# The second half's down-projection as seven-product pairs: three layers of a transformer-like encoder step on one Trainium2 core

## Chip, cores and metric

One NeuronCore of one Trainium2 chip runs the whole program. The metric is the device time of one execution in microseconds (us). TensorE (PE) multiplies, VectorE (DVE) and ScalarE (ACT) prepare its operands and read its results, GpSimd (POOL) adds a few squares, and SyncE (SP) issues nearly all transfers. Each engine works through its own queue in program order and waits on semaphores.

## The reference

Four layers over 512 prompt tokens and 32 sample tokens (544 rows of width 1024), in float32. Each layer has a token mixer (gated linear attention, band attention, a recurrent block, gated linear attention), then a SwiGLU feed-forward part; both add to x:

```python
def rmsnorm(x, g):
    y = xf * lax.rsqrt(jnp.mean(xf * xf, axis=-1, keepdims=True) + EPS)
    return (y * g.astype(jnp.float32)).astype(x.dtype)

def swiglu_ffn(x, w_in, w_out):          # w_in 1024 x 5632, w_out 2816 x 1024
    g, u = jnp.split(x @ w_in, 2, axis=-1)
    return (jax.nn.silu(g) * u) @ w_out
...
for i in range(DEPTH):                   # 4 layers
    ...                                  # xp = xp + mixer(rmsnorm(xp))
    xp = xp + swiglu_ffn(rmsnorm(xp, ffn_norms[i]), *ffn_params[i])
    xs = xs + swiglu_ffn(rmsnorm(xs, ffn_norms[i]), *ffn_params[i])
y_prompt = rmsnorm(xp, final_norm)
```

## The kernel before

**Layout.** Activations lie transposed: x is 8 tiles of 128 features by 544 tokens, a token row being two halves of 272 columns. Every matmul has a 128x128 weight tile and 272 columns. A product in float32 is made of three: each operand is split into a high part and a low rest, and hi*hi, hi*lo and lo*hi are added up. ACT writes the high part of weights (`w_hi`), DVE the low one (`w_lo`).

**The feed-forward part.** The 22 tiles of the hidden width are done in two halves of FH = 11: up-projection of half 0 (`up0`), down-projection (`down0`), then `up1` and `down1`. h is the product silu(g) * u; ACT writes `h_hi`, DVE `h_lo`. `up1` is made of eleven "seven" pairs already: a pair (u and g of one hidden tile) is a 2x2 matrix product over 2x4 input tiles and two column halves, done in Winograd's form, with 7 products of KQ = 4 tiles instead of 8. It needs sums of weight tiles (`w_sums` on DVE, then `lo_sums`, `lo_a11`, `lo_more_sums`, `lo_rest`; `hi_...` on ACT) and sums of input tiles (`t_sum`, `t_low` on DVE, `t_high` on ACT), made once for the layer. `h_low` stands in DVE's queue behind `product`, which waits for ACT's silu.

**The down-projection.** `project_out` does 8 blocks, one for each tile m of x, of 11 tiles x 3 products x 2 halves = 66 matmuls. Block b writes `slot[b % 2]` in PSUM. Ahead of a block ACT and DVE split its weights (`split`, L772 and L1483); behind it DVE multiplies by rstd (L2133), adds to x (L2136), ACT squares x (L790) and writes `xg_hi` (L775), POOL adds up the squares (L3031), and DVE writes `xg_lo` (L1495). Behind the eighth block DVE adds the last square (`last_square`, L1490), and PE's next block, the first of the next mixer, stops after six of its eight input tiles for the ten small matmuls of `stat_sum` (L2466), which wait for that sum. In the layer ahead of the second gated linear attention this first block has 4 matmuls a tile (L2422), elsewhere 6 (L2414).

**Queues.** A block's `pe.wait_ge(s_free, b - 1)` keeps PE from writing a PSUM slot that is not yet read; the semaphores are counters, so an engine that is late in its queue holds up all that waits for a later count. Weights come by SP through two `raw` buffers (and `ffn_raw_b` for every other pair).

## Time and profile before

| | |
|---|---|
| median of 3 runs | 2532.9 us (2532.87 to 2533.35) |
| profiled execution, its own time | 2532.84 us |
| its span (first to last instruction) | 2531.1 us |
| around the span | 1.7 us |
| PE busy | 2513.2 us (99%), 19925 matmuls |
| DVE busy | 1749.3 us (69%) |
| ACT busy | 1210.6 us (48%) |
| POOL busy | 166.1 us (7%) |
| share of PE in the chain that ended last | 96% |

The span is the profiler's, from the first to the last instruction of that one execution; a difference in its time is a difference in the median as far as the two agree, here within 0.1 us. Busy shares are means over stages that have different limits.

### The profile page before, as it was taken

What the parts mean: (1) busy time and instruction counts of PE and PEld (TensorE: products, weight loads), DVE (VectorE), ACT (ScalarE), POOL (GpSimd) and SP (SyncE); (2) the same over time, 40 slices, a digit from 0 to 9 for tenths busy, and PEclk for the clock granted to TensorE, in tenths of its full rate; (3) what the DMA queues carried; (4) which work ended last, traced back from release to release, by engine and by line L of the source; (5) the groups of instructions that cost most, each with busy time, mean ns of one, the idle gap of its engine ahead of it and who ended that gap; (6) DMA issues with size and microseconds to landing.
All of it is one profiled execution on the core that took longest, in us unless ns stands there. A gap on an engine that the chain in (4) does not pass through costs nothing.

```text
span 2531.1 us, 48151 instructions
## 1 busy us (share of the span) xinstructions
PE 2513.2 (99%) x19925; PEld 2451.8 (97%) x19925; DVE 1749.3 (69%) x2585; ACT 1210.6 (48%) x1831; POOL 166.1 (7%) x180
## 2 busy tenths in 40 slices
PE   9999999999999999999999999999999999999998
PEld 8999999999988899999998899999999999999998
DVE  6655994985555599489557557948955565984973
ACT  6554651543555565245245545524534554642543
POOL 1101000001000010000122110000011101000001
PEclk9999999999999999999999999999999999999999
DMA  4222333332433233333222233332323223333332
GB/s 120 71 78 84 101 101 91 100 97 82 120 96 110 71 109 95 97 97 94 85 68 74 72 92 90 103 100 84 96 82 88 72 70 92 108 89 93 106 88 78
DMA packets 443891, 230.69 MB, mean 91 GB/s; under 512 B 17092, under 2 KB 440736, under 8 KB 443696
## 3 DMA queue, kind: packets, MB, share of 16 engines
q1 hardware_dynamic: 442048, 226.90, 31.2%
q8 instruction: 140, 2.29, 0.4%
q10 hardware_dynamic: 1200, 0.59, 0.1%
q0 software_dynamic: 448, 0.45, 0.1%
q14 instruction: 55, 0.45, 0.1%
HBM read 219.03 MB, written 8.87 MB: 90 GB/s over the span
## 4 chain that ended last, share of the span: by engine, by line
PE 96%; DVE 2%; issue 1%; ACT 0%; DMA 0%; POOL 0%; SPq 0%; DVEq 0%; ACTq 0%; POOLq 0%
PE slot L2414 32%; PE slot L2457 21%; PE aux L2934 6%; PE aux L2929 6%; PE aux L2931 6%; PE slot L2934 5%; PE slot L2929 5%; PE slot L2931 5%; PE aux L2373 2%; PE aux L2827 1%; PE aux L2582 1%; PE aux L2833 1%; PE aux L2739 1%; PE aux L2677 1%; PE aux L2597 1%
## 5 line engine op out<-in xcount | busy, mean ns | idle before, releaser
L772 ACT ACTIVATE w_hi<-raw 128x1024 fp32r<-128x1024 f32 (+3 forms) x207 | 239.5, 1157 | 266.1 <-PE slot L2457 136.4
L2414 PE MATMUL slot<-xg_hi,w_hi 128*128 128x272 f32 x1664 | 361.5, 298 | 2.9 <-DVE w_lo L1483 2.9
L2414 PE MATMUL slot<-xg_lo,w_hi 128*128 128x272 f32 x1664 | 343.8, 288 | 0.0
L2414 PE MATMUL slot<-xg_hi,w_lo 128*128 128x272 f32 x1664 | 343.7, 288 | 0.0
L1483 DVE TENSOR_TENSOR w_lo<-raw,w_hi 128x1024 fp32r<-128x1024 f32 (+4 forms) x207 | 281.6, 1360 | 61.1 <-ACT w_hi L772 59.3
L2414 PEld LDWEIGHTS slot<-xg_hi,w_hi 128*128 128x128 f32 x1664 | 260.4, 189 | 14.1 <-issue 6.9
L2414 PEld LDWEIGHTS slot<-xg_lo,w_hi 128*128 128x128 f32 x1664 | 261.5, 189 | 0.0
L2414 PEld LDWEIGHTS slot<-xg_hi,w_lo 128*128 128x128 f32 x1664 | 260.4, 189 | 0.0
L2133 DVE TENSOR_TENSOR ffn_y<-slot,rstd 128x544 f32<-128x544 f32 x56 | 40.6, 724 | 194.1 <-PE slot L2457 177.9
L3031 POOL TENSOR_TENSOR sq_sum<-sq_sum,sq_x 128x544 f32<-128x544 f32 x48 | 67.9, 1414 | 1608.5 <-ACT sq_x L790 1608.2
L2457 PE MATMUL slot<-h_hi,w_hi 128*128 128x272 f32 x1078 | 150.0, 287 | 0.0
L2457 PE MATMUL slot<-h_hi,w_lo 128*128 128x272 f32 x1078 | 149.8, 287 | 0.0
L2457 PE MATMUL slot<-h_lo,w_hi 128*128 128x272 f32 x1078 | 149.8, 287 | 0.0
L790 ACT ACTIVATE sq_x<-x 128x544 f32<-128x544 f32 (+1 forms) x55 | 36.2, 658 | 222.3 <-DVE x L2136 119.4
L2457 PEld LDWEIGHTS slot<-h_hi,w_hi 128*128 128x128 f32 x1078 | 140.5, 188 | 0.0
L2457 PEld LDWEIGHTS slot<-h_lo,w_hi 128*128 128x128 f32 x1078 | 140.1, 188 | 0.0
L2457 PEld LDWEIGHTS slot<-h_hi,w_lo 128*128 128x128 f32 x1078 | 140.0, 188 | 0.0
L2934 PE MATMUL aux<-ffn_t_hi,w_lo 128*128 128x272 f32 x704 | 116.7, 287 | 0.0
L1311 ACT ACTIVATE w_hi<-ffn_w_sums 128x1024 fp32r<-128x1024 f32 x80 | 85.0, 1063 | 66.0 <-DVE ffn_w_sums L2170 64.9
L2929 PE MATMUL aux<-ffn_t_hi,w_hi 128*128 128x272 f32 x704 | 116.6, 287 | 0.0
L2931 PE MATMUL aux<-ffn_t_lo,w_hi 128*128 128x272 f32 x704 | 116.6, 287 | 0.0
L1329 ACT ACTIVATE w_hi<-ffn_w_sums 128x1024 fp32r<-128x1024 f32 x80 | 85.0, 1063 | 62.1 <-PE aux L2934 29.6
(421 smaller groups left out, 5763.3 us busy)
## 6 DMA issues: line engine op xcount, KB each, us to landing
raw<-in_l_ffn_w_out_dram SPq DMA_DIRECT2D x64, 704.0 KB, 4.6
raw<-in_l_ffn_w_in_dram SPq DMA_DIRECT2D x52, 512.0 KB, 5.0
raw<-in_l_gla_w_in_dram SPq DMA_DIRECT2D x47, 512.0 KB, 3.8
ffn_raw_b<-in_l_ffn_w_in_dram SPq DMA_DIRECT2D x88, 256.0 KB, 3.4
ffn_raw_b<-in_l_ffn_w_in_dram SPq DMA_DIRECT2D x44, 512.0 KB, 5.2
raw<-in_l_ffn_w_in_dram SPq DMA_DIRECT2D x72, 256.0 KB, 3.3
raw<-in_l_att_w_qkv_dram SPq DMA_DIRECT2D x24, 512.0 KB, 3.7
raw<-in_l_lru_w_in_dram SPq DMA_DIRECT2D x24, 512.0 KB, 3.8
```

What stands on the lines that cost most here:

```text
L772: act.activation(w_hi[par][:, 0:kt, :], raw[par][:, 0:kt, :], ACT.Copy).then_inc(s_hi, 1)
L1311: act.activation(tiles8(w_his, w_slots(b % 2)[0]), tiles8(FF["s"], 0), ACT.Copy).then_inc(s_wh, 1)
L1329: act.activation(tiles8(w_his, min(w_slots(b % 2)[2:4])), tiles8(FF["s"], 2 * KQ), ACT.Copy).then_inc(s_wh, 1)
L1483: dve.tensor_tensor(w_lo[par][:, 0:kt, :], raw[par][:, 0:kt, :], w_hi[par][:, 0:kt, :].bitcast(F32), ALU.subtract).then_inc(s_lo, 1)
L2133: dve.tensor_tensor(FF["y"][:, 2 * j:2 * j + 2, :], slot[(p0 + j) % 2][:, :, 0:HALF], halves(rstd[:, :]), ALU.mult).then_inc(s_free, 1)
L2373: return pe.transpose(out, in_, ident[rows, rows])
L2414: ins = pe.matmul((slot[par] if bank is None else bank)[:, hf, 0:HALF], w[par][:, k, :], a[:, k0 + k, hf * HALF:(hf + 1) * HALF], start=(k ...
L2457: ins = pe.matmul(to[:, hf, 0:HALF], w[par][:, k, :], a[:, k, cols], start=(k == 0 and at == 0), stop=(k == kt - 1 and at == 2))
L2929: pe.matmul(to, w_his[:, w_at + k, :], hi(k), start=(start and k == 0), stop=False, skip_group_check=True)
L2931: pe.matmul(to, w_his[:, w_at + k, :], lo(k), start=False, stop=False, skip_group_check=True)
L2934: ins = pe.matmul(to, w_los[:, w_at + k, :], hi(k), start=False, stop=(stop and k == KQ - 1), skip_group_check=True)
L3031: pool.tensor_tensor(sq_sum[:, :], sq_sum[:, :], sq_x[par][:, :], ALU.add).then_inc(s_xad, 1)
```

## The change

In layers 0, 1 and 2 the second half's down-projection (`down1`) keeps blocks 0 and 1 as they are and does blocks 2 to 7 as three seven-product pairs (blocks 2+3, 4+5, 6+7). Of the 11 hidden tiles KX = 3 are multiplied plainly and the other 8 in Winograd's form. Its input sums are made of h itself, so `product` leaves the seven h tiles 3 to 9 in float32 in places that are free in `up1` (`whole_h`), and tile 10 in `ffn_y`. All three pairs use the same two PSUM slots; the rests of the weights (`extra`) lie in the last two tiles of `xg_hi` and `xg_lo`.

```diff
+H_SUM_AT, T_DVE, T_ACT = (0, 3, 7, 11), 32, 12
+DOWN_PAIRS = (2, 4, 6)
+KX = FH - XT
...
             # ScalarE
+            def project_seven(i, b0):
...
+                split(b0 + 1, 1 - p0, FH)
+                t_half(i, 0)
+                t_half(i, 1)
+                t_half(i, 2)
+                hi_sums(pairs[0], b2, None)
+                t_half(i, 3)
+                hi_more_sums(pairs[0], b2, None)
+                hi_extra(pairs[0], b2)
+                hi_a11(pairs[0], b2, None)
+                hi_rest(pairs[0], b2)
+                copy_product(pairs[0], p0, "d")
+                copy_product(pairs[0], p0, "b")
+                x_ready(0)
+                x_ready(1)
...
+                copy_product(pairs[2], p0, "b")
+                x_ready(4)
+                x_ready(5)
+                split(b0 + 8, p0, next_k(i, "down1"))
+                x_ready(6)
+                x_ready(7)
...
             # VectorE
+            def down_ends(at, b):
+
+                n, ab = s_no[at], up_banks(at[1], at[2], b % 2)[1]
+                dve.wait_ge(s_mm, b + 2)
+                dve.wait_ge(s_out7, 5 * n + 3)
+                dve.tensor_tensor(FF["y"][:, 3, :], ab[:, 1, 0:HALF], down_v[:, :], ALU.add).then_inc(s_out7, 1)
+                dve.tensor_tensor(FF["y"][:, 0, :], ab[:, 0, 0:HALF], rstd[:, 0:HALF], ALU.mult).then_inc(s_free, 1)
+                dve.wait_ge(s_out7, 5 * n + 4)
+                dve.tensor_tensor(FF["y"][:, 2:4, :], FF["y"][:, 2:4, :], halves(rstd[:, :]), ALU.mult).then_inc(s_out7, 1)
...
+            def h_sum(i, q):
+
+                at, tq = T_DVE * i + 16 + H_SUM_AT[q], FF["hs"][:, :, q, :]
+                top, low = whole_h(i, 1, KX + q), whole_h(i, 1, KX + KQ + q)
+                dve.tensor_tensor(tq[:, 1, :], low[:, 1, :], top[:, 1, :], ALU.subtract)
+                dve.tensor_tensor(tq[:, 0, :], top[:, 0, :], top[:, 1, :], ALU.subtract).then_inc(s_tdve, 1)
+                dve.wait_ge(s_tdve, at + 1)
+                dve.scalar_tensor_tensor(tq[:, 2, :], low[:, 1, :], -1.0, tq[:, 0, :], ALU.mult, ALU.subtract).then_inc(s_tdve, 1)
+                dve.wait_ge(s_tdve, at + 2)
+                dve.scalar_tensor_tensor(tq[:, 3, :], tq[:, 2, :], -1.0, low[:, 0, :], ALU.mult, ALU.subtract).then_inc(s_tdve, 1)
...
+                split(b0 + 1, 1 - p0, FH)
+                h_sum(i, 0)
+                h_sum(i, 1)
+                h_sum_low(i, 0)
+                h_sum(i, 2)
+                h_sum_low(i, 1)
+                h_sum(i, 3)
+                h_sum_low(i, 2)
+                w_sums(pairs[0], b2)
+                h_sum_low(i, 3)
+                lo_sums(pairs[0], b2)
+                scaled(0, b0)
+                lo_more_sums(pairs[0], b2, 2)
+                scaled(1, b0 + 1, 2)
+                lo_extra(pairs[0], b2)
+                lo_a11(pairs[0], b2, 3)
+                c_plus_d(pairs[0], p0)
+                lo_rest(pairs[0], b2)
+                added(0, b0)
+                added(1, b0 + 1, 2)
+                a_plus_b(pairs[0], p0)
+                low(0)
+                low(1)
+                w_sums(pairs[1], b2 + 2)
+                down_middle(pairs[0], b2)
+                lo_sums(pairs[1], b2 + 2)
+                lo_a11(pairs[1], b2 + 2, 2)
+                lo_more_sums(pairs[1], b2 + 2, 3)
+                down_ends(pairs[0], b2)
+                lo_rest(pairs[1], b2 + 2)
+                lo_extra(pairs[1], b2 + 2)
+                c_plus_d(pairs[1], p0)
+                down_adds(pairs[0], b2)
+                low(2)
+                low(3)
+                a_plus_b(pairs[1], p0)
...
+                split(b0 + 8, p0, next_k(i, "down1"))
+                down_middle(pairs[2], b2 + 4)
+                down_ends(pairs[2], b2 + 4)
+                down_adds(pairs[2], b2 + 4)
+                low(6)
+                last_square(norm_no(i, "down1"))
+                low(7)
...
             # TensorE
+            def seven_of_down(i, j):
...
+                pe.wait_ge(s_free, b - 1)
+                pe.wait_ge(s_tdve, T_DVE * i + 32)
+                pe.wait_ge(s_wh, 3 * n + 1)
+                times(c, slots[0], *of_t(0), True, (s_wl, 3 * n + 1))
+                times(d_, slots[1], *of_t(1), True, (s_wl, 3 * n + 1)).then_inc(s_pr, 1)
+                pe.wait_ge(s_wh, third)
+                pe.wait_ge(s_free, b)
+                times(b_, slots[2], *of_t(2), True, (s_wl, third)).then_inc(s_mm, 1)
+                pe.wait_ge(s_wh, 3 * n + 3)
+                times(a, slots[4], *of_h(KX, 0), True, (s_wl, 3 * n + 3)).then_inc(s_pr, 1)
+                pe.wait_ge(s_out7, 5 * n + 1)
+                times(c, slots[3], *of_h(KX + KQ, 1), False, (s_wl, 3 * n + 3)).then_inc(s_pr, 1)
+                pe.wait_ge(s_hi, b + 2)
+                pe.wait_ge(s_lo, b + 2)
+                rest_of(c, 0, 1, False)
+                times(d_, slots[5], *of_t(3), False, (s_lo, b + 2))
+                rest_of(d_, 1, 0, False).then_inc(s_pr, 1)
+                pe.wait_ge(s_out7, 5 * n + 2)
+                times(a, slots[6], *of_h(KX + KQ, 0), False, (s_lo, b + 2))
+                rest_of(a, 0, 0, False)
+                rest_of(b_, 1, 1, True).then_inc(s_mm, 1)
```

`times` is 3 x 4 matmuls and `rest_of` 3 x 3, so a pair has 7 x 12 + 4 x 9 = 120 where two blocks have 132. `scaled(m)` is the multiplication by rstd, `added(m)` the addition to x, `low(m)` the write of `xg_lo`, `x_ready(m)` ACT's square and `xg_hi`. SP loads a pair's weights by three transfers and a fourth for the rests.

VectorE's queue between the h of the last up pair and the first read of block 0 (layer 0, `down1`; `h_sums` hold the sums of h). Before:

```order
L2256 TENSOR_TENSOR h_lo<-ffn_y,h_hi 128x544 [waits h_hi]
L2144 UNCONDITIONAL_BRANCH
L2144 ISA
L1483 TENSOR_TENSOR w_lo<-raw,w_hi 128x1408 [waits w_hi]
L2129 REGISTER_ALU
L2133 TENSOR_TENSOR ffn_y<-slot,rstd 128x544 [waits block_done]
```

Now, the last rows ahead of that read (the fourth `h_sum`, then `w_sums`, `h_sum_low(3)`, `lo_sums`, `scaled(0)`):

```order
L2398 TENSOR_TENSOR ffn_h_sums<-ffn_y,whole_in_xg_lo 128x272
L2399 TENSOR_TENSOR ffn_h_sums<-whole_in_xg_lo 128x272
L2401 SCALAR_TENSOR_TENSOR ffn_h_sums<-ffn_y,ffn_h_sums 128x272 [waits t_dve]
L2403 SCALAR_TENSOR_TENSOR ffn_h_sums<-ffn_h_sums,ffn_y 128x272 [waits t_dve]
L2408 TENSOR_TENSOR ffn_t_lo<-ffn_h_sums,ffn_t_hi 128x4x272 [waits t_act]
L2304 TENSOR_TENSOR ffn_w_sums<-ffn_raw_b 128x1024 [waits seven_raw_b_in]
L2307 TENSOR_TENSOR ffn_w_sums<-ffn_w_sums,ffn_raw_b 128x512 [waits seven_w_sums]
L2309 TENSOR_TENSOR ffn_w_sums<-ffn_w_sums,ffn_raw_b 128x512 [waits seven_w_sums]
L2408 TENSOR_TENSOR ffn_t_lo<-ffn_h_sums,ffn_t_hi 128x4x272 [waits t_act]
L2315 TENSOR_TENSOR w_lo<-ffn_w_sums,w_hi 128x1024 [waits seven_w_hi]
L2421 TENSOR_TENSOR ffn_y<-slot,rstd 128x544 [waits block_done]
```

Between the weight split and the first read of a PSUM slot there were no rows of work; now there are 24.

ScalarE's queue at the same place (the copy behind the h of the last up pair, then the split of block 1's weights). Now:

```order
L1495 ACTIVATE h_hi<-ffn_y 128x544 [waits ffn_h]
L840 ACTIVATE w_hi<-raw 128x1408 [waits block_done,raw_in0]
L1419 ACTIVATE ffn_t_hi<-ffn_h_sums 128x4x272 [waits t_dve] x3
L1379 ACTIVATE w_hi<-ffn_w_sums 128x1024 [waits block_done,seven_w_sums]
L1419 ACTIVATE ffn_t_hi<-ffn_h_sums 128x4x272 [waits t_dve]
L1397 ACTIVATE w_hi<-ffn_w_sums 128x1024 [waits block_done,seven_w_sums]
```

Before, the square of x stood directly behind the split; now the fourth copy of the h sums stands behind a copy that waits for VectorE's weight sums.

## Rows read from the trace of the kernel before

**Rows 1.** The page, part 1: busy time, share of the span and instructions.

```profile
PE 2513.2 (99%) x19925; PEld 2451.8 (97%) x19925; DVE 1749.3 (69%) x2585; ACT 1210.6 (48%) x1831; POOL 166.1 (7%) x180
```

**Rows 2.** Chain that ended last, in order of time: start us, us, what.

```profile
556.19 8.25 PE slot L2414 x66
564.44 57.41 PE slot L2457 x462
```

**Rows 3.** The same chain in 545 to 640 us, two of its pieces.

```profile
546.23 0.50 PE aux L2931 x4
...
555.21 0.49 PE aux L2931 x4
```

**Rows 4.** Timeline of DVE, 555 to 640 us: start us, us, engine line op.

```profile
559.26 0.73 DVE L2256 TENSOR_TENSOR h_lo<-ffn_y,h_hi 128x544 fp32r<-128x544 f32 x1 [0.72 <-ACT h_hi L1363]
560.53 1.63 DVE L1483 TENSOR_TENSOR w_lo<-raw,w_hi 128x1408 fp32r<-128x1408 f32 x1 [0.54 <-ACT w_hi L772]
```

**Rows 5.** Timeline of DVE, 252 to 300 us (`t_sum`, `t_low`, `w_sums`, `lo_sums` in `up0`).

```profile
268.63 0.72 DVE L2266 TENSOR_TENSOR ffn_tq<-ffn_xq 128x544 f32<-128x544 f32 x1
269.39 0.44 DVE L2269 SCALAR_TENSOR_TENSOR ffn_tq<-ffn_xq,ffn_tq 128x272 f32<-128x272 f32 x1
...
270.22 0.72 DVE L2266 TENSOR_TENSOR ffn_tq<-ffn_xq 128x544 f32<-128x544 f32 x1
...
274.26 2.50 DVE L2276 TENSOR_TENSOR ffn_t_lo<-ffn_tq,ffn_t_hi 128x1088 fp32r<-128x1088 f32 x2
276.67 1.22 DVE L2170 TENSOR_TENSOR ffn_w_sums<-ffn_raw_b 128x1024 f32<-128x1024 f32 x1
...
279.25 0.72 DVE L2340 TENSOR_TENSOR ffn_y<-slot,rstd 128x544 f32<-128x544 f32 x1
279.89 1.22 DVE L2181 TENSOR_TENSOR w_lo<-ffn_w_sums,w_hi 128x1024 fp32r<-128x1024 f32 x1
```

**Rows 6.** Timeline of ACT, 252 to 300 us: a copy of input sums, one of weight sums.

```profile
262.83 1.12 ACT L1379 ACTIVATE ffn_t_hi<-ffn_tq 128x1088 fp32r<-128x1088 f32 x1 [0.59 <-DVE ffn_tq L2271]
...
277.92 1.06 ACT L1311 ACTIVATE w_hi<-ffn_w_sums 128x1024 fp32r<-128x1024 f32 x1 [2.70 <-DVE ffn_w_sums L2170]
```

**Rows 7.** The page, part 6: transfers, KB each, us from issue to landing.

```profile
ffn_raw_b<-in_l_ffn_w_in_dram SPq DMA_DIRECT2D x44, 512.0 KB, 5.2
```

**Rows 8.** Timeline of DVE, 555 to 640 us, behind the last block of `down1`.

```profile
621.89 0.72 DVE L2133 TENSOR_TENSOR ffn_y<-slot,rstd 128x544 f32<-128x544 f32 x1 [2.86 <-PE slot L2457]
...
624.10 0.73 DVE L1490 TENSOR_TENSOR sq_sum<-sq_sum,sq_x 128x544 f32<-128x544 f32 x1 [0.72 <-ACT sq_x L790]
```

**Rows 9.** Timeline of ACT there: the last square and the last `xg_hi`.

```profile
623.41 0.66 ACT L790 ACTIVATE sq_x<-x 128x544 f32<-128x544 f32 x1 [5.95 <-DVE x L2136]
623.97 0.73 ACT L775 ACTIVATE xg_hi<-x,vec_a 128x544 fp32r<-128x544 f32 x1
```

**Rows 10.** Timeline of POOL, 540 to 650 us: its last addition of squares.

```profile
615.94 1.36 POOL L3031 TENSOR_TENSOR sq_sum<-sq_sum,sq_x 128x544 f32<-128x544 f32 x1 [6.46 <-ACT sq_x L790]
```

**Rows 11.** Timeline of PE, 619 to 650 us: `stat_sum`.

```profile
626.20 1.17 PE L2466 MATMUL aux<-mean_x,sq_sum 128*128 128x1 f32 x10
```

**Rows 12.** Stages: us, PE, PEld, DVE, ACT, POOL busy (x), PEclk, DMA share, GB/s.

```profile
572.60:621.70 49.10, 49.10 (x398) 49.10 (x397) 25.01 (x24) 15.10 (x18) 8.20 (x6) 1.00 0.30 85
...
2525.00:2528.00 3.00, 0.53 (x5) 0.29 (x4) 1.11 (x3) 1.56 (x3) 0.00 (x0) 0.80 0.37 113
2528.00:2531.00 3.00, 0.00 (x0) 0.00 (x0) 0.00 (x0) 0.00 (x0) 0.00 (x0) 0.50 0.74 294
```

**Rows 13.** Timeline of PE at the program's start and at its end.

```profile
4.73 0.24 PE L2373 MATMUL slot<-ident,gain_rows 8*128 8x8 f32 x1 [4.73 <-DMA x_rows<-in_x_sample_dram]
...
10.55 0.65 PE L2414 MATMUL slot<-xg_lo,w_hi 128*128 128x272 f32 x2
11.00 0.49 PE L2414 MATMUL slot<-xg_hi,w_lo 128*128 128x272 f32 x2
...
2522.48 0.28 PE L2891 MATMUL slot<-h_hi,w_lo 128*128 128x256 f32 x1
```

More of the change, by code:

```diff
@@ L178, in up_plan @@
                     n += 1
+        for j in range(len(DOWN_PAIRS) if i < layers - 1 else 0):
+            number[i, "down", j], buffer[i, "down", j] = n, "BA"[j % 2]
+            n += 1
     return number, buffer, h_count
@@ L1294, in raw_used @@
                     for par in range(2):
[L1295 removed]
+                        raw_off[par] -= 0 if at[1] == "down" and par == b % 2 else 16
                 else:
@@ new lines, in h_sum_low, with project_seven, scaled, added @@
+            def h_sum_low(i, q):
+                dve.wait_ge(s_tact, T_ACT * i + 8 + q + 1)
+                dve.tensor_tensor(one4(FF["t_lo"], q), one4(FF["hs"], q), one4(FF["t_hi"], q).bitcast(F32),
+                                  ALU.subtract).then_inc(s_tdve, 1)
+            def project_seven(i, b0):
+                p0, norm = b0 % 2, norm_after(i, "down1")
+                b2, pairs = b0 + DOWN_PAIRS[0], [(i, "down", j) for j in range(len(DOWN_PAIRS))]
+                def scaled(m, b, at=0):
+                    dve.wait_ge(s_mm, b + 1)
+                    if m > 1:
+                        dve.wait_ge(s_xd, XT * (2 * i + 1) + m)
+                    dve.tensor_tensor(FF["y"][:, at:at + 2, :], slot[b % 2][:, :, 0:HALF], halves(rstd[:, :]), ALU.mult).then_inc(s_free, 1)
+                def added(m, b, at=0):
+                    dve.wait_ge(s_free, b + 1)
+                    dve.tensor_tensor(one(x, m), FF["gu"[at // 2]], one(x, m), ALU.add).then_inc(s_xd, 1)
+                def add(m, b):
+                    scaled(m, b)
+                    added(m, b)
+                def low(m):
+                    xg_split(m, norm, m + split_tiles(i, "down1"))
+                split(b0 + 1, 1 - p0, FH)
[34 more added lines that the diff above has]
+                a_plus_b(pairs[1], p0)
+                w_sums(pairs[2], b2 + 4)
+                down_middle(pairs[1], b2 + 2)
+                lo_sums(pairs[2], b2 + 4)
+                lo_a11(pairs[2], b2 + 4, 2)
+                lo_more_sums(pairs[2], b2 + 4, 3)
+                down_ends(pairs[1], b2 + 2)
+                lo_extra(pairs[2], b2 + 4)
+                lo_rest(pairs[2], b2 + 4)
+                c_plus_d(pairs[2], p0)
+                down_adds(pairs[1], b2 + 2)
+                low(4)
+                low(5)
+                a_plus_b(pairs[2], p0)
+                split(b0 + 8, p0, next_k(i, "down1"))
[5 more added lines that the diff above has]
+                low(7)
@@ L2962, in project_out, with project_seven @@
+            def project_seven(i, b0, ready):
+                p0, hi, lo = b0 % 2, FF["h_hi"], FF["h_lo"]
+                mm_block(b0, p0, FH, hi, lo, ready=ready, free=b0 - 2)
+                whole_block(b0 + 1, 1 - p0, FH, hi, lo, free=b0 - 2)
+                for j in range(len(DOWN_PAIRS)):
+                    seven_of_down(i, j)
             def project_out(b0, kt, hi, lo, ready, free=None):
```

207 lines of the change are left out of this document (178 added, 29 removed).

## The prediction

> **What bounds the kernel now.** I read the page's busy shares first: PE is busy for 99% of the span, VectorE for 69%, ScalarE for 48% [rows 1]. Such a share is a mean over stages, so I went to the chain of work that ended last: in layer 0's `down1` it is PE alone, 66 matmuls in 8.25 us and then 462 in 57.41 us, without a piece of any other engine [rows 2]. In that stage VectorE is busy for 25.0 of 49.1 us [rows 12]. So PE's matmuls set the time, and fewer of them are worth their full price, as long as the other engines deliver in time. Whether they do is the question of this change, because it gives VectorE and ScalarE much more to do in exactly this stage, and part of it can't start before the last tile of h is there.
>
> **What PE saves.** A plain block's matmul takes 57.41 / 462 = 0.1243 us. One in the seven-product form takes 0.1247 us: from the piece at 546.23 to that at 555.21 are 18 pieces of 4, 8.98 us for 72 [rows 3]. Two plain blocks are 132 x 0.1243 = 16.40 us. A pair is 84 x 0.1247 + 36 x 0.1243 = 14.95 us (the 36 of `rest_of` priced like plain ones). That saves 1.45 us a pair, and 9 pairs (three in each of three layers) save **13.1 us**.
>
> **What the first pair waits for.** Blocks 0 and 1 have 132 matmuls, so PE could start the first pair at 556.19 + 8.25 + 66 x 0.1243 = 572.6. Its first matmul waits for three things: all 16 tiles of h sums (`s_tdve`), the first weight sums (`s_wh`), and the read of block 0 out of the slot it writes (`s_free`), which is `scaled(0)`. That read stands in VectorE's queue behind all four `h_sum`, all four `h_sum_low`, `w_sums` and `lo_sums`. I walk down that queue with durations of before.
>
> VectorE writes the last `h_lo` at 559.26 and starts the split of block 1's weights at 560.53 [rows 4]. Nothing of this moves earlier. An operation's successor starts about 0.08 us ahead of the end of its record: the one at 279.25, of 0.72, is followed at 279.89 [rows 5]. So the first `h_sum` can start at 562.07.
>
> An `h_sum` is a `t_sum` whose first operation, 544 wide, is cut into two of 272. A `t_sum` takes 1.59 us from start to start, its first part 0.76 of it [rows 5]. Two operations of 272 take 0.36 + 0.48 in its place (0.44 each, the second waited for), which makes 1.67 us. Four are 6.7 us. An `h_sum_low` is a `t_low`: 2.41 us for two, 1.2 each [rows 5]. Three stand ahead of `w_sums`, 3.6 us. ScalarE's copies of 1.12 us [rows 6] fit between, since each has the next `h_sum` to hide under. `w_sums` starts at 562.07 + 6.7 + 3.6 = 572.4, so VectorE alone has already used up the time of blocks 0 and 1.
>
> Then comes the knot. ScalarE's queue has `hi_sums` ahead of the fourth `t_half`. `hi_sums` waits for the first weight sum, 1.22 us behind 572.4, and takes 1.06 [rows 5, 6]: until 574.7. The fourth `t_half` takes 1.12: until 575.7. VectorE has finished `w_sums` by 575.0 and waits; its fourth `h_sum_low` runs to 577.0, `lo_sums` to 578.1 (1.22 less 0.08), and `scaled(0)` ends 0.72 later, at 578.8 [rows 5]. PE starts then, 6.2 us late. Layers 1 and 2 have the same two lists of instructions, so this is 3 x 6.2 = **18.6 us lost**, more than the pairs save. The second and third waits of the first pair (`scaled(1)`, `c_plus_d`, `lo_rest`) come out 1.3 us or more ahead of PE by the same walk.
>
> **What the other pairs wait for.** Loading is not it, I think: the second pair's transfers are issued behind the first pair's `lo_extra` at about 581.4 by the walk, some 6.5 us ahead of its `w_sums`, and such a transfer lands within 5.2 us [rows 7]; the others have more room. Per pair VectorE has, in us by the widths of rows 5: `w_sums` 2.6, `down_middle` 1.5, `lo_sums` with `lo_a11` and `lo_more_sums` 2.9, `down_ends` 1.4, `lo_rest` 1.1, `lo_extra` 0.9, `c_plus_d` and `a_plus_b` 0.7, the additions 1.3, two `xg_lo` 1.5. That is 13.9 of a pair's 14.95 us. It fits, with little air. Walking down the queue, `c_plus_d` of the third pair is the tightest: PE wants it 48 matmuls, 6.0 us, into the pair, and it is ready about 0.6 us earlier, because it stands behind `down_ends`, which can't start before the pair ahead has ended. I take 0 for these waits and keep them as a rival.
>
> **What the next layer waits for.** Before, the eighth block's product is scaled from 621.89 on (call it E), and its square is added by 624.10 + 0.73, E + 2.9 [rows 8]. PE comes to `stat_sum` at 626.20, E + 4.3, so it doesn't wait [rows 11]. Now tiles 6 and 7 of x are both finished behind E. `down_ends` has two operations of 272 and one of 544, then two additions of 544: x6 is there at E + 2.1, x7 at E + 2.7. ScalarE squares x6 until E + 2.8 (0.66), writes its `xg_hi` (0.73) and squares x7 until about E + 4.0 [rows 9]. POOL must add the square of x6, 1.36 us [rows 10], until E + 4.2; before, its last addition was done at 617.30, long ahead. VectorE's `last_square` then ends at E + 5.0. Where PE arrives at E + 4.3 (layers 1 and 2) it waits 0.7 us. Ahead of layer 3 the first block has 4 matmuls a tile and not 6, so PE arrives after 24 and not 36 of them, at E + 3.0, and waits 2.0 us. Together **3.4 us**. The splits for the second block are ready in time in both.
>
> **What TensorE's clock does.** In this trace PE rests nowhere in mid-program, and the granted clock is 1.00, the level of 2.4 GHz, in the stage [rows 12]. It falls at the very end: after the last dense matmul at 2522.48 [rows 13] PE has hardly any work, and the granted clock is 0.80 in 2525 to 2528 and 0.50 (1.2 GHz) from there on [rows 12]. A mean of 0.80 is 0.50 for 1.2 of these 3 us, so it fell about 4.3 us behind the last dense matmul. The new wait of 6.2 us is longer. What comes after such a rest is seen at the start, by durations alone: PE's first work is at 4.73, and the two matmuls at 10.55 are still 0.225 us apart [rows 13], not 0.125; the slow part is over by about 11.3, 6.6 us in. Half of the time at the lower level is lost. So a wait costs from nothing (the clock stays) to 3.3 us more. PE had gaps at the start and will have none here, so I expect a shorter slow part and take 2.0 us, 3 x 2.0 = **6.0 us**. The Trainium skill, page "TensorE: Matmul & The Clock Gate", section on the HAM clock gate, says that the array falls to the lower clock when it idles and gets the higher one back by sustained matmuls. The rows at both ends agree with it. By that page this change pays for each rest twice; without it the sum would be 6.0 us lower.
>
> **Sum.** 18.6 - 13.1 + 3.4 + 6.0 = +14.9 us, **2547.8 us**. The profiled execution has 2532.84 us by its own clock, 1.7 more than its span, and the median is 2532.9, so I add to the median directly.
>
> **Rivals.** About 0.2% (5 us) is what a measurement of this kernel can tell from no change.
> - *The clock stays up* through a rest of 6 us. For: the gap at the end was not quite a rest, with six small matmuls in it, and the level fell only once PE was all but done. Against: the slow start. Time: 2541.8 us. Chance 0.19.
> - *The pairs starve VectorE's queue.* If the 0.6 us of air in `c_plus_d` is not there and the second and third pair each lose 1 us, that is 6 us more: 2554 us. For: 13.9 of 14.95 us. Against: the other waits of a pair have 0.8 to 2 us of air by the same walk. Chance 0.14.
> - *The h sums are hidden* (faster). If VectorE's and ScalarE's chain from 562.07 to `scaled(0)` took 10.5 us in place of 16.7, the first pair would start on time and the time would be 2532.9 - 13.1 + 3.4 = 2523.2 us. It decides at a wait of (13.1 - 3.4) / 3 = 3.2 us a layer; below that, the change gains. For: only that I may have misjudged which operation must be ahead of which; the widths are those of rows 5. Chance 0.08.
> - My forecast, wait and lower clock: 0.57, own range 2543 to 2551.4 (the two ends of the clock's price are 2541.8 and 2551.7). What is left, 0.02, is a wait of half the size.
>
> **Range and chances.** From 2540 us (the clock stays up and VectorE is a little quicker) to 2554 us (the second rival): it leaves out the hidden sums and half of the starved pairs. Slower by over 0.2%, above 2538.0: 0.88. Within 0.2%: 0.04. Faster, below 2527.8: 0.08.
>
> **What will show it.** In the profile after, in each of three layers, PE should have one idle stretch of about 6 us ahead of the first `ffn_t_hi` matmul of `down1`, released by VectorE's read of `slot`; the last of the four copies of h sums on ScalarE should start about 1.1 us after a copy of `w_sums`; the granted clock should be under 1.00 just behind the stretch, with matmuls 0.225 us apart for some 4 us; a pair should then take 14.95 us without a wait; and `stat_sum` should wait 0.7, 0.7 and 2.0 us for `sq_sum`. The count of matmuls must fall by 108. I am wrong if the stretch is under 3.2 us, or if the later pairs are longer than 15.5 us.

## The result, and the profile after

The changed kernel takes 2557.6 us (median of 4 runs, 2556.2 to 2558.1) against 2533.1 us (2532.9 to 2533.4) of the kernel before beside it: a ratio of 1.0096, 95% interval 1.0084 to 1.0108. It is 24.5 us slower. The direction is as forecast, the size is not: 2547.8 us was predicted and 2554 us was the upper end of the range.

The profiled execution has 2558.13 us by its own clock, 25.3 more than the one of before. Its page, part 1, answers to [rows 1]:

```profile
PE 2513.9 (98%) x19817; PEld 2449.7 (96%) x19817; DVE 1841.6 (72%) x2762; ACT 1246.1 (49%) x1897; POOL 167.7 (7%) x180
```

TensorE has 108 matmuls fewer and is not busy for less: at half the clock a matmul is busy for longer. What it waits for, from the view of waits (us in total, times, longest):

```profile
PE slot L3251 <- DVE ffn_y L2421: 18.4, 3, 6.2
...
PE aux L2746 <- DVE sq_sum L1624: 4.6, 3, 2.5
...
PE slot L3251 <- DVE ffn_y L2382: 0.8, 3, 0.3
```

The first row is the wait ahead of the first pair, for `scaled(0)`. The timelines of VectorE, ScalarE and TensorE in layer 0 show what is late there (start us, us, engine line op; for the durations of before see [rows 5] and [rows 6]):

```profile
572.64 1.22 DVE L2304 TENSOR_TENSOR ffn_w_sums<-ffn_raw_b 128x1024 f32<-128x1024 f32 x1
...
575.98 1.29 DVE L2408 TENSOR_TENSOR ffn_t_lo<-ffn_h_sums,ffn_t_hi 128x1088 fp32r<-128x1088 f32 x1 [0.67 <-ACT ffn_t_hi L1419]
577.19 1.22 DVE L2315 TENSOR_TENSOR w_lo<-ffn_w_sums,w_hi 128x1024 fp32r<-128x1024 f32 x1
578.33 0.72 DVE L2421 TENSOR_TENSOR ffn_y<-slot,rstd 128x544 f32<-128x544 f32 x1
...
573.89 1.06 ACT L1379 ACTIVATE w_hi<-ffn_w_sums 128x1024 fp32r<-128x1024 f32 x1 [4.08 <-DVE ffn_w_sums L2304]
574.85 1.09 ACT L1419 ACTIVATE ffn_t_hi<-ffn_h_sums 128x1088 fp32r<-128x1088 f32 x1
...
579.10 1.28 PE L3251 MATMUL slot<-ffn_t_hi,w_hi 128*128 128x272 f32 x4 [6.11 <-DVE ffn_y L2421]
```

`w_sums` starts at 572.64, and TensorE's last matmul of block 1 ends at 572.99. VectorE later stands for 0.67 us, because ScalarE does a copy of weight sums ahead of the last copy of h sums, and reads block 0 at 578.33.

The stages of the granted clock answer to [rows 12]. The first three lines begin where TensorE's work starts again behind the 6 us wait in layers 0, 1 and 2, the last three lie behind `stat_sum` (us, PE, PEld, DVE, ACT, POOL busy (x), PEclk, DMA share, GB/s):

```profile
579.10:584.00 4.90, 4.90 (x24) 4.90 (x25) 3.24 (x5) 0.09 (x1) 0.00 (x0) 0.56 0.21 62
1236.50:1243.00 6.50, 6.45 (x31) 6.45 (x32) 3.50 (x6) 0.54 (x2) 0.00 (x0) 0.56 0.42 119
1880.30:1884.00 3.70, 3.67 (x16) 3.67 (x17) 3.27 (x5) 0.12 (x1) 0.00 (x0) 0.52 0.02 4
634.00:638.60 4.60, 4.60 (x26) 4.60 (x26) 0.79 (x2) 1.58 (x3) 0.00 (x0) 0.63 0.14 52
1293.00:1297.00 4.00, 4.00 (x23) 3.99 (x21) 0.00 (x0) 1.06 (x1) 1.85 (x3) 0.57 0.50 140
1934.50:1938.40 3.90, 3.90 (x22) 3.90 (x22) 1.10 (x2) 1.30 (x3) 0.84 (x2) 0.57 0.54 153
```

TensorE's busy time multiplied by what the clock lacks to 1.00 is taken as the loss. Behind the first pair's wait that is 4.90 x 0.44 + 6.45 x 0.44 + 3.67 x 0.48 = 6.8 us. And the clock falls a second time in each layer, behind `stat_sum`: 4.6 x 0.37 + 4.0 x 0.43 + 3.9 x 0.43 = 5.1 us. The prediction has no such term. TensorE's timeline there, layer 0, answers to [rows 11]:

```profile
632.91 1.28 PE L2746 MATMUL aux<-mean_x,sq_sum 128*128 128x1 f32 x10 [1.06 <-DVE sq_sum L1624]
...
635.10 0.65 PE L2694 MATMUL slot<-xg_hi,w_hi 128*128 128x272 f32 x2
635.55 0.66 PE L2694 MATMUL slot<-xg_lo,w_hi 128*128 128x272 f32 x2
```

A rest of 1.06 us, ten matmuls of one column, and soon after that two matmuls take 0.45 us from start to start: the level of 1.2 GHz. The ten are part of what stands ahead of the fall. The kernel before, too, has a rest in mid-program, a longer one, which the prediction overlooked ("PE rests nowhere in mid-program"). It is followed at once by matmuls of 272 columns, and the stage behind it keeps the full clock:

```profile
1342.61 0.52 PE L2414 MATMUL slot<-xg_hi,w_hi 128*128 128x272 f32 x2 [1.56 <-DVE w_lo L1483]
```

```profile
1342.60:1346.60 4.00, 3.99 (x25) 3.69 (x26) 3.93 (x6) 0.77 (x2) 0.70 (x2) 1.00 0.48 135
```

The last piece is the third pair. By the timeline of TensorE the second pair takes 596.10 to 611.07, 14.97 us, and the third until 627.19, 16.12 (16.04 and 16.05 in layers 1 and 2):

```profile
596.10 0.66 PE L3251 MATMUL slot<-ffn_t_hi,w_hi 128*128 128x272 f32 x4
...
611.07 0.66 PE L3251 MATMUL slot<-ffn_t_hi,w_hi 128*128 128x272 f32 x4
611.57 0.66 PE L3253 MATMUL slot<-ffn_t_lo,w_hi 128*128 128x272 f32 x4
612.24 0.76 PE L3256 MATMUL slot<-ffn_t_hi,w_lo 128*128 128x272 f32 x4
...
614.76 0.74 PE L3251 MATMUL slot<-ffn_t_hi,w_hi 128*128 128x272 f32 x4 [0.27 <-DVE ffn_y L2382]
...
623.31 0.78 PE L3251 MATMUL slot<-h_hi,w_hi 128*128 128x272 f32 x4
...
627.19 0.41 PE L2694 MATMUL slot<-xg_hi,w_hi 128*128 128x272 f32 x2
```

VectorE and GpSimd at that time:

```profile
603.56 3.22 DVE L1629 SCALAR_TENSOR_TENSOR xg_lo<-x,vec_a,xg_hi 128x544 fp32r<-128x544 f32 x2 [0.78 <-ACT xg_hi L843]
...
610.97 1.22 DVE L2315 TENSOR_TENSOR w_lo<-ffn_w_sums,w_hi 128x1024 fp32r<-128x1024 f32 x1
...
613.84 0.43 DVE L2381 TENSOR_TENSOR ffn_y<-slot,down_v 128x272 f32<-128x272 f32 x1
...
622.83 0.43 DVE L2362 TENSOR_TENSOR down_u<-slot,down_u 128x272 f32<-128x272 f32 x1
...
602.97 1.36 POOL L3376 TENSOR_TENSOR sq_sum<-sq_sum,sq_x 128x544 f32<-128x544 f32 x1 [12.59 <-ACT sq_x L858]
604.84 1.36 POOL L3376 TENSOR_TENSOR sq_sum<-sq_sum,sq_x 128x544 f32<-128x544 f32 x1 [0.50 <-POOL sq_sum L3376]
```

Two `xg_lo` take 3.22 us, and GpSimd's additions of squares lie over them. TensorE then stops at three places of the third pair, in each layer: at 612.24 for `lo_sums` (610.97), at 614.76 for the read in `down_ends` (L2382, behind 613.84, which comes 2.8 us after the second pair's end), and at 623.31 for `a_plus_b` (622.83). For `c_plus_d` it never waits.

The balance, from the profiled executions:

| part | predicted | measured | from |
|---|---|---|---|
| wait ahead of the first pair | +18.6 | +18.4 | waits, 3 x 6.1 to 6.2 |
| clock behind it | +6.0 | +6.8 | stages |
| matmuls saved | -13.1 | -13.1 | 108 fewer; second pair 14.97 us |
| third pair | 0 | +3.4 | 16.12 + 16.04 + 16.05 - 3 x 14.95 |
| wait at `stat_sum` | +3.4 | +4.6 | waits |
| clock behind `stat_sum` | not in the sum | +5.1 | stages |
| sum | +14.9 | +25.2 | the executions differ by 25.3 |

The rows on waits and on the clock are each a little off, and the errors nearly cancel. A matmul of 272 columns at the lower level takes 0.225 us in place of 0.125, so it loses 0.44 of its time, while the granted clock lacks 0.50. By the starts of matmuls the three falls behind `stat_sum` cost 4.3 us and not 5.1 (1.5 us for one, by the comparison with the first experiment below), and a rest costs 0.16 us more than its idle time. Below, a fall is still priced at 1.7 us where the granted clock is the source.

### The profile page after: what moved, and what is told of

The parts are those of the page before. It is cut to its first block and busy times, and to the rows that moved or that the text cites. A ratio compares the mean times of both kernels' runs of the same rounds, so it can differ in the third digit from the quotient of the medians.

```text
span 2556.4 us, 47977 instructions
## 1 busy us (share of the span) xinstructions
PE 2513.9 (98%) x19817; PEld 2449.7 (96%) x19817; DVE 1841.6 (72%) x2762; ACT 1246.1 (49%) x1897; POOL 167.7 (7%) x180
## 5 line engine op out<-in xcount | busy, mean ns | idle before, releaser
L840 ACT ACTIVATE w_hi<-raw 128x1024 fp32r<-128x1024 f32 (+4 forms) x189 | 214.9, 1137 | 267.7 <-PE slot L2737 136.4
L1617 DVE TENSOR_TENSOR w_lo<-raw,w_hi 128x1024 fp32r<-128x1024 f32 (+4 forms) x189 | 252.4, 1335 | 59.4 <-ACT w_hi L840 57.8
L1379 ACT ACTIVATE w_hi<-ffn_w_sums 128x1024 fp32r<-128x1024 f32 x89 | 94.6, 1063 | 97.6 <-DVE ffn_w_sums L2304 96.5
L1397 ACT ACTIVATE w_hi<-ffn_w_sums 128x1024 fp32r<-128x1024 f32 x89 | 94.4, 1060 | 61.2 <-PE slot L3214 29.1
L2267 DVE TENSOR_TENSOR ffn_y<-slot,rstd 128x544 f32<-128x544 f32 x32 | 23.2, 725 | 138.0 <-PE slot L2737 128.7
L2329 DVE TENSOR_TENSOR w_lo<-ffn_w_sums,w_hi 128x1024 fp32r<-128x1024 f32 x89 | 108.3, 1217 | 0.4
L2315 DVE TENSOR_TENSOR w_lo<-ffn_w_sums,w_hi 128x1024 fp32r<-128x1024 f32 x89 | 108.1, 1215 | 0.0
L3209 PEld LDWEIGHTS aux<-ffn_t_hi,w_hi 128*128 128x128 f32 x704 | 99.4, 188 | 0.0
L1629 DVE SCALAR_TENSOR_TENSOR xg_lo<-x,vec_a,xg_hi 128x544 fp32r<-128x544 f32 (+1 forms) x56 | 70.7, 1274 | 39.8 <-ACT xg_hi L843 39.8
L3214 PEld LDWEIGHTS aux<-ffn_t_hi,w_lo 128*128 128x128 f32 x704 | 99.2, 188 | 0.0
L3211 PEld LDWEIGHTS aux<-ffn_t_lo,w_hi 128*128 128x128 f32 x704 | 99.0, 188 | 0.0
```

The source lines that it names most:

```text
L840: act.activation(w_hi[par][:, 0:kt, :], raw[par][:, 0:kt, :], ACT.Copy).then_inc(s_hi, 1)
L1379: act.activation(tiles8(w_his, w_slots(b % 2)[0]), tiles8(FF["s"], 0), ACT.Copy).then_inc(s_wh, 1)
L1397: act.activation(tiles8(w_his, min(w_slots(b % 2)[2:4])), tiles8(FF["s"], 2 * KQ), ACT.Copy).then_inc(s_wh, 1)
L1617: dve.tensor_tensor(w_lo[par][:, 0:kt, :], raw[par][:, 0:kt, :], w_hi[par][:, 0:kt, :].bitcast(F32), ALU.subtract).then_inc(s_lo, 1)
L1629: dve.scalar_tensor_tensor(one(xg_lo, m), one(x, m), gain(norm, m), one(xg_hi, m).bitcast(F32), ALU.mult, ALU.subtract).then_inc(s_xlo, 1)
L2315: dve.tensor_tensor(tiles8(w_los, to), tiles8(FF["s"], 0), tiles8(w_his, to).bitcast(F32), ALU.subtract).then_inc(s_wl, 1)
```

## The experiments

All stand against the kernel before on the same chip, whose medians beside them were 2533.2 to 2533.4 us. Three questions had to be told apart: what makes the third pair and `stat_sum` late, whether a wait of 1 us really is enough to bring the clock down, and whether the entry and the end of the projection cost each for itself.

**GpSimd's additions cut to 8 columns** (layers 0 to 2; most of the sum of squares is left out, so this kernel's results are other numbers):

```diff
-                    pool.tensor_tensor(sq_sum[:, :], sq_sum[:, :], sq_x[par][:, :], ALU.add).then_inc(s_xad, 1)
+                    n = TOK if cols is None else cols
+                    pool.tensor_tensor(sq_sum[:, 0:n], sq_sum[:, 0:n], sq_x[par][:, 0:n], ALU.add).then_inc(s_xad, 1)
...
-                x_norm_sum(norm_no(i, "down1"))
+                x_norm_sum(norm_no(i, "down1"), cols=8 if i < last else None)
```

> The changed kernel, with GpSimd's additions of squares in the second down-projection of layers 0 to 2 cut to 8 of 544 columns (most of the sum of squares is left out, so rstd of the next norm is another number; every wait and every instruction stays). Theory A (GpSimd's additions stretch VectorE's xg_lo from 0.78 us to 1.2 to 1.6 us, which makes the third pair late): the xg_lo of rows like 603.56 take 0.78 us, the third pair lasts 14.95 us again instead of 16.12 (3.5 us less over three layers), the wait at stat_sum shrinks below its 1.06, 1.05 and 2.52 us, and the time is about 2552 us; if the wait shrinks so far that the clock does not fall behind it, up to 5 us less still. Rival B (xg_lo is long for a reason of its own, its operands or VectorE's queue): its median stays near 1.35 us and the time stays within 1 us of 2557.6.

Measured: 2549.9 us (2549.5 to 2552.4), 7.7 less than the changed kernel. The groups of VectorE and GpSimd in 595 to 632 us (xcount | busy us, mean ns | idle before):

```profile
L1629 DVE SCALAR_TENSOR_TENSOR xg_lo<-x,vec_a,xg_hi 128x544 fp32r<-128x544 f32 x6 | 4.7, 784 | 3.1 <-ACT xg_hi L843 3.1
...
L3377 POOL TENSOR_TENSOR sq_sum<-sq_sum,sq_x 128x8 f32<-128x8 f32 x5 | 1.1, 223 | 39.0 <-ACT sq_x L858 39.0
```

In the changed kernel the same group has a mean of 1583 ns:

```profile
L1629 DVE SCALAR_TENSOR_TENSOR xg_lo<-x,vec_a,xg_hi 128x544 fp32r<-128x544 f32 x5 | 7.8, 1583 | 2.3 <-ACT xg_hi L843 2.3
```

Theory A holds: `xg_lo` takes twice its time only while GpSimd adds 544 columns. The third pair takes 14.98 us in each layer, the three waits on L2382, 0.8 us in all, are gone from the view of waits, `stat_sum` waits 2.9 us in place of 4.6, and the clock doesn't fall behind it in this execution. The parts would be worth 3.4 + 1.7 + 5.1 = 10.2 us, and the profiled executions differ by 8.2 (2549.9 to 2558.1). Of the rest, 0.6 us came back behind the first pairs' waits, where the clock cost 7.4 us in this execution, and 0.3 us in a longer first transfer (5.4 us for 5.1). Another 0.8 us is the price of the falls: from the ten matmuls of `stat_sum` to the next first pair (in layer 3 to a matmul at its end) the two executions differ by 1.5, 1.2 and 1.5 us, less than the 1.7 us each that were counted. The Trainium skill, page "GPSIMD Engine Reference", section 8, Key points, says that GpSimd shares its SBUF interfaces with VectorE and contends with its instructions that have two SBUF inputs. `xg_lo` has two, x and `xg_hi`, and this pair of traces agrees, with 784 against 1583 ns.

**`stat_sum` one block later:**

```diff
-                hooks = {SUM_AT: lambda: stat_sum(k, mean_x)}
+                late = i > 0 and k == stat_of[i, "mix"]
+                hooks = {} if late else {SUM_AT: lambda: stat_sum(k, mean_x)}
...
-                mm_block(b0 + 1, 1 - p0, XT, xg_hi, xg_lo, hooks={SPREAD_AT: lambda: stat_spread(k)})
+                hooks = {SPREAD_AT: lambda: stat_spread(k)}
+                if late:
+                    hooks = {2 * low: lambda: stat_sum(k, mean_x), 2 * low + 2: lambda: stat_spread(k)}
+                mm_block(b0 + 1, 1 - p0, XT, xg_hi, xg_lo, hooks=hooks)
```

> The changed kernel, with stat_sum behind the second down-projection of layers 0 to 2 moved from the seventh k of the next projection's first block to the head of its second block (up to 3.5 us later), so that VectorE's last_square is in time; rstd then comes 3 us later. Theory A (the wait at stat_sum, 4.6 us in all, and the fall of the granted clock to 1.2 GHz behind it, 1.7 us in each of three layers, are both real losses of TensorE): both go, if the later rstd makes nobody late, and the time falls by 8 to 10 us to about 2548 us. Rival B (the clock falls because of the ten small matmuls of stat_sum themselves or of the transition between projections, not because of the wait): the wait goes but the fall stays, and only 4 to 4.6 us are saved (2553). Rival C (rstd is needed at once by VectorE's queue, which is behind anyway): the saved wait comes back at the next eviction, and the time stays near 2557.

Measured: 2555.6 us (2554.8 to 2557.8), 2.0 less by the medians, with runs that overlap those of the changed kernel (2556.2 to 2558.1). The wait only changed its name. The view of waits:

```profile
PE slot L2702 <- DVE xg_lo L1629: 2.5, 2, 1.9
...
PE slot L2694 <- DVE xg_lo L1629: 1.4, 4, 0.4
```

With 0.4 us more for `w_lo` that is 4.3 us, for 4.6 before. The seventh and eighth `xg_lo` are as late as the sum of squares, and TensorE needs them in the same block. The rests now are two short ones in layers 0 and 1 (0.42 and 0.32 us), and the clock stays up there; ahead of layer 3 there are three, of 1.89, 0.59 and 0.40 us with a few wide matmuls between, and behind them it falls (1.6 us lost), here ahead of the ten small matmuls. Two falls fewer at 1.7 us and 0.3 us less of waiting would be 3.7 us; that the median fell by only 2.0 is not traced. Theory A's part on the wait and rival C were each half right: what is late is VectorE behind the third pair, not one instruction.

**The order of the knot:** `t_half(i, 3)` ahead of `hi_sums` on ScalarE, `h_sum_low(i, 3)` ahead of `w_sums` on VectorE.

```diff
                 t_half(i, 2)
+                t_half(i, 3)
                 hi_sums(pairs[0], b2, None)
-                t_half(i, 3)
...
+                h_sum_low(i, 3)
                 w_sums(pairs[0], b2)
-                h_sum_low(i, 3)
```

> The changed kernel with the fourth t_half ahead of the first pair's hi_sums on ScalarE and h_sum_low(3) ahead of w_sums on VectorE. Theory A (the wait of 6.1 us ahead of the first pair is the length of VectorE's queue, t_sum to a11, of which only the 0.67 us idle at 575.98 come from ScalarE's order): the wait falls by 0.6 to 0.7 us in each of three layers, about 2 us in all, to 2555.6 us. Rival B (the wait hangs on ScalarE's copies, in whose row w_hi would now come 1.1 us later): the wait grows by 0.4 us or more in each layer and the time rises by over 1 us.

Measured: 2556.3 us (2555.1 to 2557.8), 1.3 less by the medians, with overlapping runs; what shows the effect is the wait. It shrank by 0.7 us a layer:

```profile
PE slot L3251 <- DVE ffn_y L2421: 16.3, 3, 5.5
```

Theory A, as far as the wait goes. ScalarE's order is a tenth of it; the rest is the length of VectorE's own queue.

**Delays in the kernel before.** Here nothing of the change is present: the kernel before gets additions of 544 columns, results unused, ahead of `last_square`.

```diff
+DELAYS = [4, 3, 1, 0]
...
                         if norm and isinstance(m, int) and m == XT - 1:
+                            for n in range(DELAYS[i] if name == "down1" else 0):
+                                dve.tensor_tensor(FF["y"][:, 0:2, :], halves(rstd[:, :]), halves(rstd[:, :]), ALU.add).then_inc(s_delay, 1)
+                                dve.wait_ge(s_delay, sum(DELAYS[0:i]) + n + 1)
                             last_square(norm_no(i, name))
```

> The kernel before, with four, three and one additions of 544 columns (0.7 us each, results unused) on VectorE ahead of last_square in the second down-projection of layers 0, 1 and 2, so that stat_sum has to wait for about 1 us with nothing else changed: no pairs in this down-projection, no wait of 6 us ahead of them. Theory A (about 1 us of waiting at stat_sum is enough for the granted clock to fall to 1.2 GHz behind it, for some 3 us): waits of 0.7 to 1.6 us in three places, 3 to 4 us in all, each followed by matmuls 0.225 us apart for about 3 us, which costs 1.7 us more each: the time rises by 3.5 + 5 us to about 2541.5 us. Rival B (the fall comes from what TensorE or the chip did before in the changed kernel, for instance the 6 us wait 50 us earlier): no fall, only the waits: about 2536.5 us.

Measured: 2535.4 us (2534.3 to 2536.4). The dose was too small: only layer 0 waited, 0.75 us, and the clock stayed up. That doesn't tell the theories apart. (The profiled execution also lost 1.8 us near the program's start: a group of matmuls that begins at 45.21 us in the kernel before begins at 47.01.) The next has five additions in each layer.

> As e4_before_delay, which gave one wait of 0.7 us with no fall of the clock behind it, now with five additions in each of layers 0 to 2: from e4's rows a wait at stat_sum of about 1.4, 1.4 and 2.9 us. Theory A (a rest of over 1 us of TensorE here is enough for the clock to fall behind it): 5.7 us of waits and 1.7 us lost by the clock in each layer, 2544 us. Rival B (only what the changed kernel does before the boundary makes it fall): waits alone, 2539 us. Rival C (it falls behind some of the waits and not behind others, as e1_no_pool, where 2.0 us of rest cost nothing, suggests): between, with 1.7 us for each fall that the profile shows.

Measured: 2544.3 us (2543.8 to 2545.4), within 0.4 us of theory A. TensorE's timeline at `stat_sum` in the three layers:

```profile
628.13 1.28 PE L2471 MATMUL aux<-mean_x,sq_sum 128*128 128x1 f32 x10 [1.51 <-DVE sq_sum L1492]
...
1280.83 1.28 PE L2471 MATMUL aux<-mean_x,sq_sum 128*128 128x1 f32 x10 [1.51 <-DVE sq_sum L1492]
...
1919.38 1.30 PE L2471 MATMUL aux<-mean_x,sq_sum 128*128 128x1 f32 x10 [3.00 <-DVE sq_sum L1492]
```

The stage behind the first of them:

```profile
630.00:634.00 4.00, 4.00 (x23) 4.00 (x22) 0.01 (x1) 1.06 (x1) 0.00 (x0) 0.57 0.32 95
```

In a program whose clock is 1.00 everywhere else in mid-program, three rests of 1.5, 1.5 and 3.0 us, with the ten small matmuls behind them, bring it down to 1.2 GHz, at 4.0 x 0.43 = 1.7 us each. 6.0 us of waits and 5.1 of clock are the 11.1 us measured. So the second fall belongs to this place and its wait, not to what the pairs did earlier. It doesn't belong to the length of the rest alone: the same profile has the 1.55 us rest for `w_lo` at 1349.06, ahead of wide matmuls, and the granted clock behind it is 1.00. Nor to the ten small matmuls alone: in the kernel before they come without a rest at three places, and no fall follows.

**How short may the rest be?** Four, four and two additions.

> As e8_before_more_delay (waits of 1.5, 1.4 and 3.0 us, the clock fell behind each), with four, four and two additions instead of five: waits of about 0.7, 0.7 and 0.8 us at stat_sum. Theory A (there is a length of rest below which the clock stays up, and it lies between the 0.7 us of e4, no fall, and the 1.06 us of the changed kernel, a fall each time): no fall in any of the three, and 2.2 us of waits: 2535.5 to 2536 us. Rival B (e4's single wait without a fall was chance): at least one of the three falls, 1.7 us more for each, up to 2541 us.

Measured: 2538.6 us (2536.4 to 2541.0), above both figures of theory A. `stat_sum` waits 0.75, 0.75 and 0.73 us, and the stages behind are these:

```profile
629.00:633.00 4.00, 4.00 (x34) 3.88 (x33) 1.18 (x2) 1.33 (x2) 0.00 (x0) 1.00 0.16 53
1280.00:1284.00 4.00, 4.00 (x21) 4.00 (x21) 0.55 (x2) 1.32 (x2) 1.57 (x2) 0.57 0.47 133
```

Rival B holds: the same rest with the same ten matmuls behind it cost nothing in layer 0 and 1.7 us in layer 1. The runs are 4.6 us apart from lowest to highest, where those of the kernel before are 2. That fits a number of falls that differs from execution to execution, but only one was profiled, and the program's start alone, up to that group of matmuls, differs by up to 1.8 us between profiles.

**The kernel of the first experiment once more.**

> The same kernel as e1_no_pool (most of the sum of squares left out), looked at once more, since its 2.0 us rest of TensorE at the last stat_sum had no fall of the clock behind it, against all eight others of 1.06 us and over. Theory A (whether a rest of this length is followed by a fall varies from execution to execution): the profile shows the same waits of 0.5, 0.5 and 2.0 us, and a fall behind the 2.0 us one is about as likely as not; with it the time is some 1.7 us above e1's 2549.9. Rival B (something in this kernel, such as the idle GpSimd, keeps the clock up): no fall again.

Measured: 2551.9 us. The same rest of 1.98 us stands at the same place. The stage behind it in the first profiled execution, and in this one:

```profile
1928.00:1932.00 4.00, 4.00 (x33) 3.79 (x33) 1.55 (x3) 2.33 (x4) 0.07 (x1) 1.00 0.53 149
```

```profile
1928.00:1932.00 4.00, 4.00 (x22) 4.00 (x23) 1.54 (x3) 1.88 (x4) 0.59 (x2) 0.57 0.47 121
```

Theory A: one kernel, one rest, and once the clock falls and once it doesn't; the time is 2.0 us longer with the fall. Between the same two matmuls (from 1926.98 to 2468.14, and from 1927.48 to 2470.18) it is 1.5 us longer. One of the four runs of the first experiment took 2552.4 us as well.

**Other places for the pairs.** Three kernels have two pairs in `down1` and four plain blocks, with the weights' loads and the two queues put in order for it. Each line is `DOWN_PAIRS` of one of them; the two that begin with a later block also have `split` and the plain `whole_block` for blocks 2 (and 3) ahead of the first pair.

```diff
-DOWN_PAIRS = (2, 4, 6)
+DOWN_PAIRS = (4, 6)
+DOWN_PAIRS = (2, 4)
+DOWN_PAIRS = (3, 5)
```

> Plain blocks 0 to 3, seven-product pairs for 4 and 5 and for 6 and 7: four blocks of lead instead of two for what VectorE prepares, and the end of the projection as in the changed kernel. Theory A (the two costs are separate: 25 us at the entry, 10 us at the boundary): the entry's wait and its fall of the clock go, the boundary keeps 1.1, 1.1 and 2.5 us of wait or less and up to 1.7 us of clock each, and two pairs save 6 x 1.45 us: 2533.4 - 8.7 + 9.7 = 2534.4 us, or 2529.5 if the clock stays up. Rival B (VectorE's queue is too full for pairs wherever they stand): the wait ahead of the first pair stays at 2 us or more in each layer and the time is above 2541.

Measured: 2535.4 us (2534.8 to 2539.6). The entry's wait is down to 1.2 us in all, its fall is gone, `stat_sum` waits 4.6 us as in the changed kernel, with a fall behind each in the profile. The profiled execution is one of the slower ones (2537.3 us); seven of the ten runs took 2534.8 to 2535.8 us, and what they lacked is not known.

> Seven-product pairs for blocks 2 and 3 and for 4 and 5, blocks 6 and 7 plain: the entry as in the changed kernel, the end as in the kernel before. Theory A: the first pair waits 6.1 us in each layer and the clock falls behind it, 25 us in all; no wait at stat_sum beyond 0.2 us, no second fall: 2533.4 - 8.7 + 25.1 = 2549.8 us. Rival B (the boundary is late because of VectorE's backlog from the entry, not because of the last pair's sums): stat_sum still waits about 1 us and the time is 2555 us or more.

Measured: 2550.4 us (2548.9 to 2551.8). TensorE waits 6.12 us ahead of the first pair and not at all at `stat_sum`:

```profile
579.07 1.27 PE L3243 MATMUL slot<-ffn_t_hi,w_hi 128*128 128x272 f32 x4 [6.12 <-DVE ffn_y L2418]
...
631.34 1.17 PE L2738 MATMUL aux<-mean_x,sq_sum 128*128 128x1 f32 x10
```

The two costs are separate, and each is where the theory puts it. There is no fall behind `stat_sum`.

For the pairs at 3 and 5, VectorE's queue ahead of the first product reads:

```diff
...
                 split(b0 + 1, 1 - p0, FH)
                 h_sum(i, 0)
                 h_sum(i, 1)
                 h_sum_low(i, 0)
+                scaled(0, b0)
+                split(b0 + 2, p0, FH)
                 h_sum(i, 2)
                 h_sum_low(i, 1)
                 h_sum(i, 3)
                 h_sum_low(i, 2)
                 w_sums(pairs[0], b2)
                 h_sum_low(i, 3)
+                scaled(1, b0 + 1, 2)
                 lo_sums(pairs[0], b2)
...
```

> Three plain blocks, pairs for blocks 3 and 4 and for 5 and 6, block 7 plain: three blocks of lead at the entry and the plain end. Theory A (both costs go when the first pair has one more plain block ahead and the last block is plain): no wait of over 0.3 us ahead of the pairs, no fall of the clock, and the time is 2533.4 - 8.7 = 2524.7 us, up to 2 us more where GpSimd's additions stretch xg_lo. Rival B (one block of lead, 8 us, is not enough for the 13 us that VectorE and ScalarE need from t_sum to a11 with the evictions between): 2 us or more of wait in each layer, with 1 to 2 us of clock, and 2533 us or more.

Measured: 2526.3 us (2525.2 to 2528.0), ratio to the kernel before 0.9972, 95% interval 0.9961 to 0.9983: 6.9 us faster than the kernel before and 31 us faster than the changed one. Its page, part 1:

```profile
PE 2505.4 (99%) x19853; PEld 2443.4 (97%) x19853; DVE 1823.2 (72%) x2723; ACT 1239.5 (49%) x1879; POOL 170.3 (7%) x180
```

The stages of layer 0 from the first pair to the next projection:

```profile
580.00:612.00 32.00, 32.00 (x257) 31.84 (x257) 29.95 (x42) 15.71 (x25) 6.43 (x4) 1.00 0.31 86
612.00:626.00 14.00, 14.00 (x116) 14.00 (x115) 11.60 (x14) 7.29 (x10) 3.03 (x2) 1.00 0.27 76
```

TensorE is busy throughout at full clock there. VectorE, at 29.95 of 32 us, has next to nothing left in the pairs; the plain block ahead and the plain block behind are what it catches up in. Of the 1.6 us above the expectation the waits show 0.9: once 0.6 us for `w_lo` and once 0.3 us for `down_ends`. The profiled execution (2526.9 us) also starts 1.0 us later than that of the kernel before (46.24 for 45.21 at the group named above).

## Why the prediction was wrong

Its direction rested on the right step. The wait ahead of the first pair came out at 6.1 to 6.2 us for 6.2, with its knot on ScalarE as walked through; the order experiment priced the knot at 0.7 us a layer. The pairs' saving (13.1 us, 108 matmuls) and the second pair's 14.95 us stand (14.97). The clock did fall behind the wait, so the rival in which it stays up was wrong; 2.0 us a layer was 2.3. That this came so near is partly luck: the same wait was followed by a loss of 1.5 to 3.1 us in the other profiles. What failed, in the order of size:

- **"What TensorE's clock does" priced one fall a layer, and there are two.** The prediction had the second wait itself, at `stat_sum`, and read the fall at the end of the program as one that comes 4.3 us behind the last dense matmul [rows 12, 13]. From that it took a wait of 6.2 us as long enough and never asked about those of 0.7 to 2.0 us: their price was put at nothing without a reason. A single fall shows what one rest was followed by, not how short a rest may be, nor what else may stand beside it: in the delayed kernel before, 1.5 us and ten small matmuls were enough. The step also rested on a wrong reading. TensorE does rest in mid-program in the kernel before, for 1.56 us at 1342.61, and the clock stays up; so rows at hand bore on short rests, and they alone would have spoken for no fall. Worth 5.1 us. With this term the forecast would have been 2552.9.
- **"Two `xg_lo` 1.5" was mis-sized; they take 3.2 in the second and third pair.** That was in the sum of 13.9 of 14.95 us, and with 15.6 it doesn't fit. The price was the operation's width alone. In the kernel before it takes 1.22 to 1.35 us in all six blocks of the same stage (572.6 to 621.7), each time beside one of GpSimd's additions, and I did not ask what lay beside it. In the kernel before GpSimd's addition slows a VectorE that has time; here VectorE has none. Worth 3.4 us in the third pair, as the experiment without the additions showed (the pair takes 14.98 us again). So "what the other pairs wait for" is 0 for the second pair and not for the third; the rival in which the pairs starve VectorE's queue was right for one of its two pairs, by its price of about 1 us a pair. The text named `c_plus_d` of the third pair as the tightest place and gave the others 0.8 us of air or more. That was wrong: TensorE waited for `lo_sums`, for the read in `down_ends` and for `a_plus_b`, and for `c_plus_d` nowhere. In the second pair `a_plus_b` was ready at 607.13 and wanted at 607.33, so its air was 0.2 us.
- **"What the next layer waits for"** had 0.7, 0.7 and 2.0 us, and it was 1.06, 1.05 and 2.52. The missing 0.4 a layer is the same contention: `xg_lo` of tile 6 stands in VectorE's queue ahead of `last_square` with GpSimd's last addition over it. Without the additions the waits are 0.47, 0.47 and 1.98. Worth 1.2 us.
- The range's upper end, 2554, was one rival's price alone. It left out that a starved queue in the last pair and the wait at `stat_sum` have the same cause and come together.

What stays open: what decides, for one kernel and one rest, whether the clock falls. No run moved the ten small matmuls away from a rest of 1 us and left all else as it was, so their part in the fall is seen from where falls come and where they don't, and not from an experiment on them.
